# Stick-breaking attention: the turned tiles of four steps in one row on PE, with four turn banks and one score bank

## The reference, cut to what matters

```python
z = einsum('bthd,bshd->bhts', q, k) * scale          # s < t only
log_beta, log_rem = log_sigmoid(z), where(mask, log_sigmoid(-z), 0.0)
after = cumsum(log_rem, reverse=True) - log_rem
w = where(mask, exp(log_beta + after), 0.0)
o = einsum('bhts,bshd->bthd', w, v)
out = rmsnorm(x + (o * silu(g)) @ w_out)
```

## Time and profile before

| what | value |
|---|---|
| time, median of 3 runs (lowest, highest) | 1659.36 us (1658.45, 1660.88) |
| time of the profiled execution | 1659.32 us |
| its span, first to last instruction | 1657.6 us |
| PE busy | 1643.4 us, 8600 matmuls |
| weight loads of PE busy (beside PE) | 1377.7 us |
| DVE busy | 1348.4 us |
| ACT busy | 906.1 us |
| POOL busy | 166.9 us |
| granted clock of PE, mean | 0.999 |

### The profile page before, as it was taken

The page is one execution under the profiler, slowest core; times in us unless marked ns, Lnnn a source line. Parts: engine busy times, 40 slices in busy tenths (PEclk is TensorE's granted clock), DMA queues, the critical chain, the costliest instruction groups (busy, mean ns, idle before and its releaser), DMA issues.

```text
span 1657.6 us, 23401 instructions
## 1 busy us (share of the span) xinstructions
PE 1643.4 (99%) x8600; PEld 1377.7 (83%) x8600; DVE 1348.4 (81%) x1897; ACT 906.1 (55%) x1779; POOL 166.9 (10%) x200
## 2 busy tenths in 40 slices
PE   8999999999999999999999999999999999999998
PEld 7888888888888888888888888888888888888886
DVE  5536379989998989889998888998989898957874
ACT  6635245655666565656565655656565656753221
POOL 0020020110111011101110211011011101000000
PEclk9999999999999999999999999999999999999999
DMA  9858543343524252433333333424242424779732
GB/s 308 270 171 275 191 146 103 108 129 88 153 64 141 64 153 89 122 98 119 108 100 103 119 113 88 128 89 146 58 147 80 145 73 129 243 258 362 248 107 84
DMA packets 164226, 237.10 MB, mean 143 GB/s; under 512 B 49936, under 2 KB 91920, under 8 KB 164112
## 3 DMA queue, kind: packets, MB, share of 16 engines
q1 hardware_dynamic: 94624, 160.03, 30.7%
q10 hardware_dynamic: 69488, 75.58, 14.6%
HBM read 155.78 MB, written 79.76 MB: 142 GB/s over the span
## 4 chain that ended last, share of the span: by engine, by line
PE 98%; DMA 1%; ACT 0%; DVE 0%; SPq 0%; issue 0%; DVEq 0%
PE proj_ps L741 32%; PE turn_ps L768 14%; PE z_ps L759 8%; PE z_ps L758 8%; PE o_ps L783 8%; PE o_ps L782 8%; PE proj_ps L696 5%; PE turn_ps L812 4%; PE o_ps L696 3%; PE turn_ps L696 3%; PE z_ps L812 3%; PE proj_ps L812 2%; PE o_ps L812 1%; DMA gate<-gate_cols 1%; DMA a_norm_col<-in_a_norm 0%; ACT o_part_hi L971 0%
## 5 line engine op out<-in xcount | busy, mean ns | idle before, releaser
L940 ACT ACTIVATE u<-z_ps 128x512 f32<-128x512 f32 (+3 forms) x640 | 341.2, 533 | 402.1 <-PE z_ps L759 397.9
L1170 DVE TENSOR_TENSOR_SCAN u<-u,u 128x512 f32<-128x512 f32 x384 | 491.7, 1280 | 0.0
L1175 DVE TENSOR_TENSOR r_turned_lo<-turn_ps,r_turned_hi 128x512 fp32r<-128x512 f32 (+3 forms) x640 | 382.2, 597 | 107.0 <-ACT r_turned_hi L946 102.1
L946 ACT ACTIVATE r_turned_hi<-turn_ps 128x512 fp32r<-128x512 f32 (+3 forms) x640 | 340.2, 532 | 60.8 <-issue 44.4
L768 PE MATMUL turn_ps<-ident,u 128*128 128x128 f32 x2176 | 342.8, 273 | 0.0
L741 PE MATMUL proj_ps<-hT_hi,w_hi 128*128 128x512 f32 x768 | 319.9, 417 | 0.0
L741 PE MATMUL proj_ps<-hT_hi,w_lo 128*128 128x512 f32 x768 | 319.9, 416 | 0.0
L741 PE MATMUL proj_ps<-hT_lo,w_hi 128*128 128x512 f32 x768 | 319.7, 416 | 0.0
L768 PEld LDWEIGHTS turn_ps<-ident,u 128*128 128x128 f32 x2176 | 267.8, 140 | 58.8
L680 POOL TENSOR_SCALAR w_raw<-w_raw,a_norm_col 128x128 f32<-128x128 f32 x192 | 165.1, 878 | 1206.5 <-DMA w_raw<-in_w_qkg 1206.5
L759 PE MATMUL z_ps<-k_parts,q_swapped 128*128 128x512 f32 (+3 forms) x640 | 233.9, 365 | 0.0
(11 more groups left out here) (122 smaller groups left out, 1586.1 us busy)
## 6 DMA issues: line engine op xcount, KB each, us to landing
qk_hi_cols<-made_hi ACTq DMA_DIRECT2D x64, 256.0 KB, 2.9
qk_lo_cols<-made_lo ACTq DMA_DIRECT2D x64, 256.0 KB, 2.4
x_T<-in_xT SPq DMA_DIRECT2D x30, 512.0 KB, 6.1
w_raw<-in_w_qkg SPq DMA_DIRECT2D x24, 512.0 KB, 3.7
x_rows<-in_x SPq DMA_DIRECT2D x16, 512.0 KB, 5.2
v_rows<-v_stage ACTq DMA_DIRECT2D x32, 256.0 KB
v_here<-v_rows SPq DMA_DIRECT2D x64, 128.0 KB, 3.1
v_next<-v_rows SPq DMA_DIRECT2D x64, 128.0 KB, 3.4
```

The lines of the kernel that those rows point to most:

```text
L940: nc.scalar.activation(u_t[(m // CB) % RU][STEPS[m][3]][:, 0:w], z_ps[m % RZ][:, 0:w], ACT.Sigmoid, scale=-Z_SCALE).then_inc(s_u, 1)
L946: nc.scalar.activation(rt_hi[m % RT][:, 0:w], t_ps[m % RT][:, 0:w], ACT.Copy).then_inc(s_hi, 1)
L1170: nc.vector.tensor_tensor_scan(u, u, other, start, ALU.mult, op).then_inc(s_r, 1)
L1175: nc.vector.tensor_tensor(rt_lo[m % RT][:, 0:w], t_ps[m % RT][:, 0:w], as_f32(rt_hi[m % RT][:, 0:w]), ALU.subtract).then_inc(s_lo, 1)
```

## The change

On PE the turns of four steps stand in one row at the end of every fourth step: at the end of step n with (n + 1) % 4 == 0, the turns of n+1 to n+4, one whole unit. Before, each step had the turn of n+2 between scores and projections. There are four turn banks in place of three, and one score bank in place of two. The turned parts have four pairs of buffers; the place for the fourth comes from the second o stage and from a place that is free by then, so there is one o stage. On ACT, the first three high parts of a row stand ahead of the sigmoid and the fourth behind it; the other three steps have none. On DVE the low parts stand ahead of the scan: in the steps of a unit one, two, one and none. The sigmoid gets a second wait, for the scan eight steps before its own.

```diff
-AT_RT = BASE + 56 * KB
+AT_RT = [(BASE + a * KB, BASE + b * KB) for a, b in ((56, 58), (60, 62), (64, 66), (82, 92))]
-LEAD_TURN = 2
+BUNCH = 4
+LEAD_TURN = 1
 LEAD_SCAN = 6
-RU, RZ, RT, RO, RP = 3, 2, 3, 2, 2
+LOW_OF = [(0,), (0, 1), (1,), ()]
+RU, RZ, RT, RO, RP = 3, 1, 4, 1, 2
...
+def turned_at(n):
+
+    first = n + LEAD_TURN
+    return [m for m in range(first, first + BUNCH) if inside(m)] if first % BUNCH == 0 else []
...
-        row_ps = z_ps + t_ps[:2]
+        row_ps = z_ps + t_ps[:2] + t_ps[3:]
         v_ps = p_ps + [t_ps[2], o_ps]
-        y_ps = [p_ps, z_ps, t_ps[:2], [t_ps[2], o_ps]]
+        y_ps = [p_ps, z_ps + t_ps[3:], t_ps[:2], [t_ps[2], o_ps]]
...
-                        for par in range(2):
-                            sp.wait_ge(s_oout[par], 32 * 2 * LAST_G * NC // 2)
+                        sp.wait_ge(s_oout[0], 32 * 2 * LAST_G * NC)
...
                     if inside(n + LEAD_SCORES):
                         scores(n + LEAD_SCORES)
-                    if inside(n + LEAD_TURN):
-                        if n + LEAD_TURN == RT - 1:
-                            pe.wait_ge(s_vT, 1)
-                        turn(n + LEAD_TURN)
                     project(filled(n - 1), filled(n))
                     put_out(out_filled(n - 1), out_filled(n))
                     if inside(n):
                         weigh(n)
+                    for m in turned_at(n):
+                        if m == 2:
+                            pe.wait_ge(s_vT, 1)
+                        turn(m)
...
                     act.wait_ge(s_z, m + 1)
+                    if m >= (RU - 1) * CB:
+                        act.wait_ge(s_r, m - (RU - 1) * CB + 1)
...
+                    turned = turned_at(n - 1)
+                    for m in turned[:-1]:
+                        hi(m)
                     if inside(n + LEAD_SCORES):
                         stick(n + LEAD_SCORES)
+                    for m in turned[-1:]:
+                        hi(m)
                     if ended is not None:
                         store_o(ended)
-                    if inside(n + LEAD_TURN):
-                        hi(n + LEAD_TURN)
...
                         made_low(g)
+                    for m in LOW_OF[n % BUNCH]:
+                        if inside(n + m):
+                            lo(n + m)
                     if inside(n + LEAD_SCAN):
                         scan(n + LEAD_SCAN)
-                    if inside(n):
-                        lo(n)
```

More of the change, by code:

```diff
@@ L300, in all_stages @@
         u_t = [[place(nc, f"u{n}_{r}", [P, CH], F32, AT_U + 2 * KB * (CB * n + r)) for r in range(CB)] for n in range(RU)]
-        rt_hi = [place(nc, f"r_turned_hi{n}", [P, CH], F32R, AT_RT + 4 * KB * n) for n in range(RT)]
-        rt_lo = [place(nc, f"r_turned_lo{n}", [P, CH], F32R, AT_RT + 4 * KB * n + 2 * KB) for n in range(RT)]
+        rt_hi = [place(nc, f"r_turned_hi{n}", [P, CH], F32R, at[0]) for n, at in enumerate(AT_RT)]
+        rt_lo = [place(nc, f"r_turned_lo{n}", [P, CH], F32R, at[1]) for n, at in enumerate(AT_RT)]
         o_st = [place(nc, f"o_stage{n}", [P, CH], F32, AT_OST + 2 * KB * n) for n in range(RO)]
```

## The result

The changed kernel takes 1684.71 us (median of 4 runs, 1682.93 to 1686.03) against 1659.32 us (1658.45 to 1660.88): a ratio of 1.0149, 95% interval 1.0137 to 1.0162. It is 25.4 us slower; the forecast was 6 us slower, 1665.3, with a range up to 1680. Direction right, size wrong.

A forecast was written before the change was run, and what follows sets the result against it. PE was taken to bound the kernel through its own instructions and new waits. Row -12, ACT with one score bank +13, DVE's order +4 and the end +1 sum to +6 us on 1659.32: 1665.3 us, range 1649 to 1680.

The forecast's parts named there:

- PE as the bound: In attention, only PE's own instructions and new waits of PE can move the time; PE is busy all 1202.00 us.
- The gain of the row: Joining turns on PE removes part of the delay behind 480 of 640 turns: 12 us gained, bounds 5 and 17.
- The 0.04 us behind a turn: On PE, a turn delays the matmuls behind it by 0.04 us, kept as 0.02 to 0.05; 0.025 stays on average.
- that rival (forecast 0.08): On PE, the turn is not what delays matmuls behind it, so only waits are left: 1677 us; chance 0.08.
- The clock: Rival: turning matmuls in a row lower PE's clock; a tenth of the stage at 1.2 GHz gives 1780 us; chance 0.05.
- ACT and one score bank: In chunks' first units, PE's scores wait for ACT's sigmoid to empty the one score bank: +13 us, bounds 2 and 22.
- the mechanism that I priced (store, extras, a 0.1 us short slack): On ACT in 64 first-unit steps: 0.1 us lost each, 6 us, plus stores, high parts and weights, 17 us; 13 taken.
- The 96 units costed at nothing: In the units that aren't a chunk's first, ACT has 0.2 to 0.7 us left, so no waits for scores.
- DVE's order: Low parts come late behind V differences, made_lo and a scan, so PE's weighing waits: +4 us, bounds 0 and 9.
- The end: Near the end ACT carries the output weights' parts in the same steps, with one score bank: +1 us, bounds 0 and 4.
- one o stage: One o stage in place of two costs nothing, as chunks end at least four steps (8 us) apart.
- the sigmoid's added wait: On ACT, the sigmoid's new wait for a scan eight steps older is already met and costs nothing.

The follow-up runs named there:

- e5_bunch1: The changed kernel with one turn (of n+2) at the end of each step, no rows, same banks, low part ahead of the scan; 1684.64 us.
- e9_pairs: The changed kernel with rows of two turns, two score banks, three turn banks, one o stage, low parts ahead of scans; 1663.15 us.
- e2_low: The changed kernel with the second low part of a row directly behind the first, ahead of the scan between them; 1673.34 us.
- e1_one_bank: The kernel before with one score bank in attention in place of two, turns and parts where they were; 1669.20 us.
- e8_ahead: The kernel before with the low part of a step ahead of its scan and nothing else; 1660.37 us.
- e7_behind: The changed kernel with e2_low's order of low parts, but behind the scans of their steps; 1671.81 us.
- e4_both: The changed kernel with e2_low's order and the weights' high and low parts later, in steps of a row that have room; 1670.81 us.

## Why the prediction was right and wrong

**PE as the bound: right.** All of the 25.8 us is in PE's stream.

**The gain of the row: mechanism right, size off.** -12 was predicted (bounds 5 and 17), -7.5 measured. e5_bunch1 and e9_pairs put it in order: 18.2 us of small delays with one turn (those just over the line counted in), 13.9 with two, 10.9 with four. The 0.04 us behind a turn was right to read as a cost of the turn, so that rival (forecast 0.08) falls; but over all 480 joined steps it comes to 7.5/480 = 0.016, not 0.025. The scores behind a row still start 0.31 us before their successor (572.76 to 573.07), and narrow steps keep theirs, as feared.

**The clock: half right.** The rival was a clock that falls because of turns in a row. Sixteen ran at a granted 1.00 (the windows row from 571.09). It does fall, but behind long waits, twice. The Trainium skill, "TensorE: Matmul & The Clock Gate", section on the PE-mode transpose, says that the full clock doesn't engage for transposes. The trace doesn't agree: the sixteen have a granted 1.00.

**ACT and one score bank: +13 predicted, about the same measured, by another cause.** Scores held in the third and fourth step of first units, with the half clock behind them, come to 7.5 + 2.6 + 3.1 = 13.2 us. That the sum fits is luck: the mechanism that I priced (store, extras, a 0.1 us short slack) gave 13.2 - 6.5 - 3.1 = 3.6. The other 9.6 is two events that I had not priced, and the clock behind them: ACT standing for POOL at the weights' high part. The row was there: the earlier trace rows end L895 with 5.1 us of idle for POOL. With two score banks that idle was ACT's own affair; I counted instructions ahead of the sigmoid and not the waits of those instructions. The 96 units costed at nothing did give nothing on scores.

**DVE's order: the step that failed most.** +4 with a bound of 9 was predicted, 10.6 + 1.2 = 11.8 measured, and e2_low takes the 10.6 away by one line. "In a unit of 16 turning matmuls the slacks are 0.7 to 0.9 and only the 4 low parts of weights pass them" was wrong: 13 full units waited, 4.0 us. In first units 20 places took 6.6, 0.33 each, against 24 places of 0.16 and 0.42 counted one by one. The timeline at 946 shows why: a difference and a made tile's low part come in the same step, 0.45 + 0.60 us by their starts, on top of a scan, and the difference takes 0.53 there, not the 0.42 used (0.41 is its mean over all 64). In e5_bunch1 the same instructions stand in the way without a row. Slack was weighed against single instructions, not against what stands together, and not against ACT's delays, which pass on to DVE as it waits for high parts.

**The end: +1 with a bound of 4 predicted, +7.6 measured.** ACT's parts of the output weights (1.04 us each) and of the pieces (1.28) stand between sigmoids of the last 40 steps, and PE waits up to 2 us for one. By what waited, 3.7 us are scores and 3.9 weighing; at the longest wait of weighing (1.39 us, at 1459.44) DVE had itself stood 2.62 us for ACT's high part, behind output weights. e1_one_bank has 4.4 of the end without any row. **The start** was left out: 1.7 us, which e1_one_bank also has.

**Neutral as costed**: the low parts ahead of the scans (e8_ahead, e7_behind; pairs with the end spread differ by 8.3 us), one o stage (no wait for a store in attention in after's list), and the sigmoid's added wait: the waits view puts 13.5 us of ACT's idle time, 13 times, down to a scan from 231 to 1433 us, but no wait of PE begins within 2 us behind any of them.

Summed: the gain missed by 4.5, DVE's order by 7.8, the end by 6.6, the start by 1.7, the score bank by 0.2, less the 1.3 that before had: 19.5 of the 19.8 by which the attention stage missed.

Open: how much of the end's other waits is ACT's delay and how much DVE's own.

## What to carry to other kernels

A second buffer between two engines also hides what the helper itself waits for: before taking it away, list for each step every instruction between two hand-overs, with its own idle time, and sum those that stand in one step. Joining short matmul groups gave 0.016 us per group; it pays only where the helpers' deadlines have more slack than the bunch adds. A delayed helper that is moved to another step moves the wait with it, so that a rearrangement is judged by the sum of PE's waits. And a hand-over between two helpers needs steps of room too: put into one step, it makes one stand for the other and delays what PE needs behind it.

## What the runs showed of the hardware that was not expected

Behind some long waits PE ran at half its clock for about 3.4 us (1339.90 to 1343.30 in after, granted 0.50); starts of the matmuls with 512 columns are then 0.42 us apart, and one stretch costs about 1.6 us (its matmuls' ends against the distances at full clock). In attention of all runs there are eleven such stretches; each began 0.07 to 1.13 us after PE had gone on from a wait of 1.65 to 3.08 us, and five waits of that length had none. What decides it stayed open: two waits of the same length, at the same step, ended differently. The timeline of PE in e2_low, and then in e4_both:

```profile
1449.43 0.50 PE L765 MATMUL z_ps<-k_parts,q_parts 128*128 128x512 f32 x1 [2.69 <-ACT u L949]
...
1451.24 0.63 PE L765 MATMUL z_ps<-k_parts,q_parts 128*128 128x512 f32 x1
1451.66 0.63 PE L766 MATMUL z_ps<-k_parts,q_swapped 128*128 128x512 f32 x1
```

```profile
1450.01 0.50 PE L770 MATMUL z_ps<-k_parts,q_parts 128*128 128x512 f32 x1 [2.70 <-ACT u L954]
...
1451.54 0.47 PE L770 MATMUL z_ps<-k_parts,q_parts 128*128 128x512 f32 x1
1451.84 0.40 PE L771 MATMUL z_ps<-k_parts,q_swapped 128*128 128x512 f32 x1
```

POOL's multiplications of weights vary: the eight of one tile took 6.89 us in the timeline at 774.35, while the median of all 192 is 0.606 us, 4.8 for eight. That spread is what ACT's order by fixed steps can't foresee; what makes it was not tried.
